# Differential attention: mask first, the two score maps in turn, and a head norm computed in token quarters

## The reference, cut to what matters

```
S_c  = (q_c / 8) k_c^T, causal mask added,   c = 0, 1      # 1024 x 1024, q_c, k_c of width 64
p    = softmax(S_0) - lam * softmax(S_1)
o    = p @ v                                               # width 128
o_a  = o * rsqrt(mean(o*o over the 128) + 1e-6) * gain     # the head norm
y_a  = o_a * silu(z)
```

## Time and profile before

| | us |
|---|---|
| median of 3 runs | 3134.0 (3133.04 to 3135.56) |
| profiled execution, its own time | 3136.14 |
| its span in the profile | 3134.4 |
| TensorE busy | 2935.7 (94%) |
| VectorE busy | 1498.8 (48%) |
| GpSimd busy | 1200.4 (38%) |
| ScalarE busy | 794.3 (25%) |

### The profile page before, as it was taken

One profiled execution on the slowest core, in us unless ns is written; L12 is line 12 of the kernel. 1 busy time (PEld: TensorE's weight loads), 2 busy tenths in 40 slices (PEclk: granted clock), 3 DMA queues, 4 the chain that ended last, 5 costly groups with the idle time before them and its releaser, 6 DMA issues.

```text
span 3134.4 us, 38375 instructions
## 1 busy us (share of the span) xinstructions
PE 2935.7 (94%) x14298; PEld 2324.2 (74%) x14298; DVE 1498.8 (48%) x2235; ACT 794.3 (25%) x1396; POOL 1200.4 (38%) x560
## 2 busy tenths in 40 slices
PE   5899999999979999999997998998879999999997
PEld 2578888888757777777766787877758878888885
DVE  6433433433454556666555655747350134444444
ACT  3410000000053333333332223232233332211212
POOL 0254444444422422122211233334244356565554
PEclk8999999999989999999998999988889999999998
DMA  8111111111111010010100121111222221111112
GB/s 363 61 54 50 50 47 47 47 47 47 41 68 41 22 34 27 27 33 27 33 20 14 41 61 32 48 40 54 81 81 100 81 74 61 60 54 66 54 61 114
DMA packets 58221, 185.24 MB, mean 59 GB/s; under 512 B 17300, under 2 KB 17428, under 8 KB 55976
## 3 DMA queue, kind: packets, MB, share of 16 engines
q1 hardware_dynamic: 37152, 152.68, 14.3%
q10 hardware_dynamic: 21000, 31.61, 2.9%
HBM read 163.22 MB, written 21.05 MB: 59 GB/s over the span
## 4 chain that ended last, share of the span: by engine, by line
PE 81%; DVE 10%; ACT 3%; issue 3%; POOL 1%; DMA 1%; DVEq 0%; POOLq 0%; ACTq 0%; SPq 0%
PE ps L597 26%; PE ps L599 25%; PE ps L598 25%; PE ps L720 1%; PE ps L923 1%; PE ps L665 1%; DVE tree L1746 1%; DVE acc L1864 1%; DVE da_sq L2027 1%; PE ps L771 1%; PE ps L683 1%; DVE ml_t L2133 1%; PE ps L914 1%; DMA edge<-edges 1%; ACT sg_g L1696 0%
## 5 line engine op out<-in xcount | busy, mean ns | idle before, releaser
L458 POOL TENSOR_TENSOR slab_hi<-slab_raw,zero 128x1024 fp32r<-128x1024 f32 x227 | 445.3, 1962 | 1557.7 <-PE ps L599 1466.0
L597 PE MATMUL ps<-h_hi,slab_hi 128*128 128x512 f32 x2512 | 1003.7, 400 | 21.9 <-DVE h_lo L1827 15.5
L598 PE MATMUL ps<-h_lo,slab_hi 128*128 128x512 f32 x2512 | 989.6, 394 | 0.0
L599 PE MATMUL ps<-h_hi,slab_lo 128*128 128x512 f32 x2512 | 989.1, 394 | 0.0
L460 POOL TENSOR_TENSOR slab_lo<-slab_raw,slab_hi 128x1024 fp32r<-128x1024 f32 x227 | 573.0, 2524 | 17.8
L597 PEld LDWEIGHTS ps<-h_hi,slab_hi 128*128 128x128 f32 x2512 | 479.6, 191 | 124.5 <-issue 12.9
L599 PEld LDWEIGHTS ps<-h_hi,slab_lo 128*128 128x128 f32 x2512 | 478.2, 190 | 103.8
L598 PEld LDWEIGHTS ps<-h_lo,slab_hi 128*128 128x128 f32 x2512 | 479.3, 191 | 96.0 <-issue 0.2
L1864 DVE TENSOR_TENSOR acc<-ps,acc 128x512 f32<-128x512 f32 x448 | 295.0, 688 | 55.2 <-PE ps L599 53.3
L1871 DVE TENSOR_TENSOR ffn_p<-ps,ffn_g 128x1024 f32<-128x1024 f32 x22 | 26.9, 1225 | 457.0 <-PE ps L599 449.8
L1862 DVE SCALAR_TENSOR_TENSOR resid<-ps,mod,resid 128x512 f32<-128x512 f32 x320 | 212.5, 744 | 0.0
(11 more groups left out here) (296 smaller groups left out, 4043.0 us busy)
## 6 DMA issues: line engine op xcount, KB each, us to landing
slab_raw<-w_in SPq DMA_DIRECT2D x168, 512.0 KB, 3.5
mod_big<-mod_w SPq DMA_DIRECT2D x12, 2048.0 KB, 13.1
slab_raw<-w_c SPq DMA_DIRECT2D x43, 512.0 KB, 3.5
res_scr<-resid ACTq DMA_DIRECT2D x4, 2048.0 KB, 7.4
resid<-res_scr ACTq DMA_DIRECT2D x2, 4096.0 KB, 12.9
gv_scr<-sg_t ACTq DMA_DIRECT2D x16, 512.0 KB, 2.6
slab_raw<-gv_scr SPq DMA_DIRECT2D x16, 512.0 KB, 3.5
resid<-x_t SPq DMA_DIRECT2D x2, 2048.0 KB, 16.6
```

The lines of the kernel that those rows point to most:

```text
L458: pool.tensor_tensor(hi, raw[slot][:], zeros, ALU.add).then_inc(hi_done.sem, 1)
L597: pe.matmul(dst, w_h, r_h, start=first, stop=False, skip_group_check=True)
L598: pe.matmul(dst, w_h, r_l, start=False, stop=False, skip_group_check=True)
L599: return pe.matmul(dst, w_l, r_h, start=False, stop=last, skip_group_check=True)
```

## The change

- `da_scores`: both waits stand ahead of the tile; then both masks are written first (they now open the accumulation), then for each column chunk the three products, each for map 0 and at once for map 1. The signals of both maps are given by the last two matmuls.
- `da_squares`: four fp32 matmuls with 32 weight columns each, one for each quarter of the tokens; quarter g lands in partitions 32g to 32g+31 of a 256-column area (`norm_stat`: in `PS[1]`'s upper half, in the last head in `PS[2]`). It waits in addition for the value copies of the head (`a_vl`), which read that area.
- `da_root` and `da_norm` work on 128 by 256 (one reciprocal instead of two of 128 by 512).
- `da_spread` is new: four fp32 matmuls, each with one column of the identity repeated as weight, spread the scale over all partitions into the upper halves of `PS[0]` and `PS[1]` (`norm_wide`). It stands behind the first half of the next value projection, ahead of the tile pair's values, and waits for the reciprocal; in the last head's norm it stands between the halves of a projection of the next stage. `da_result` reads PSUM now.
- The wait of the first transposes for the root is gone.

```diff
@@ da_scores (TensorE)
                 cols = slice(i * P, (i + 1) * P)
+                if i >= 1:
+                    pe.wait_ge(a_exp.sem, a_exp.at(h, 2 * (i - 1)))
+                    pe.wait_ge(a_mix.sem, a_mix.at(h, i - 1))
                 for c in range(2):
-                    rows = slice(c * DA_QK, (c + 1) * DA_QK)
-                    if i >= 1 and c == 0:
-                        pe.wait_ge(a_exp.sem, a_exp.at(h, 2 * (i - 1)))
-                    elif i >= 1:
-                        pe.wait_ge(a_mix.sem, a_mix.at(h, i - 1))
-                    for t0 in range(0, (i + 1) * P, HALF):
-                        t1 = min(t0 + HALF, (i + 1) * P)
-                        three(score_bank[c][:, t0:t1], q_hi[rows, cols], q_lo[rows, cols],
-                              k_hi[rows, t0:t1], k_lo[rows, t0:t1], True, True)
-                    pe.matmul(score_bank[c][:, cols], ident_b[:], mask_b[:], start=False, stop=True,
-                              skip_group_check=True).then_inc(a_score.sem, 1)
+                    pe.matmul(score_bank[c][:, cols], ident_b[:], mask_b[:], start=True, stop=False, skip_group_check=True)
+
+                for t0 in range(0, (i + 1) * P, HALF):
+                    t1 = min(t0 + HALF, (i + 1) * P)
+                    diagonal = t1 == (i + 1) * P
+                    for n, (q, k) in enumerate(((q_hi, k_hi), (q_hi, k_lo), (q_lo, k_hi))):
+                        for c in range(2):
+                            rows = slice(c * DA_QK, (c + 1) * DA_QK)
+                            mm = pe.matmul(score_bank[c][:, t0:t1], q[rows, cols], k[rows, t0:t1],
+                                           start=(n == 0 and not diagonal), stop=(n == 2), skip_group_check=True)
+                            if diagonal and n == 2:
+                                mm.then_inc(a_score.sem, 1)
@@ da_squares, da_spread (TensorE)
-            def da_squares(h):
+            def da_squares(h, last=False):
                 pe.wait_ge(a_sq.sem, a_sq.at(h))
                 pe.wait_ge(a_o.sem, a_o.at(h))
-                for t0 in (0, HALF):
-                    mm = pe.matmul(PS[2][:, t0:t0 + HALF], ones[:], da_sq[:, t0:t0 + HALF], start=True, stop=True,
+                if not last:
+                    pe.wait_ge(a_vl.sem, a_vl.at(h + 1))
+                for g in range(4):
+                    mm = pe.matmul(norm_stat(last)[32 * g:32 * g + 32, :], ones[:, 0:32], da_sq[:, g * QUARTER:(g + 1) * QUARTER],
+                                   start=True, stop=True, skip_group_check=True)
+                mm.then_inc(a_ss.sem, 1)
+
+            def da_spread(h, last=False):
+                pe.wait_ge(a_r.sem, a_r.at(h, 0))
+                for g in range(4):
+                    dst = norm_wide(last, g // 2)[:, g % 2 * QUARTER:(g % 2 + 1) * QUARTER]
+                    mm = pe.matmul(dst, ident[:, 32 * g:32 * g + 1].to_broadcast([P, P]), da_rq[:], start=True, stop=True,
                                    skip_group_check=True)
-                mm.then_inc(a_ss.sem, 1)
+                mm.then_inc(a_r.sem, 1)
@@ da_head (TensorE)
                 da_half(h, DA_Z_SLAB, 0 if last else 1)
-                if out:
-                    pe.wait_ge(a_std.sem, a_std.at(h - 1))
                 da_turn(h, 0, 0)
...
                     da_half(h + 1, DA_V_SLAB, 0)
+                if out:
+                    da_spread(h - 1)
                 da_values(h, 0)
@@ behind the last head (TensorE)
-            da_squares(DA_HEADS - 1)
-            project(IN_ML + 1, 1)
-            pe.wait_ge(a_std.sem, a_std.at(DA_HEADS - 1))
+            da_squares(DA_HEADS - 1, last=True)
+            project(IN_ML + 1, 1, between=lambda: da_spread(DA_HEADS - 1, last=True))
@@ da_root (ScalarE)
-                act.activation(da_sq[:], PS[2], ACT.Sqrt, bias=eps[:, 0:1], scale=1.0 / DA_V).then_inc(a_std.sem, 1)
+                act.activation(da_rq[:], norm_stat(last), ACT.Sqrt, bias=eps[:, 0:1], scale=1.0 / DA_V).then_inc(a_std.sem, 1)
@@ da_norm, da_result (VectorE)
-                dve.reciprocal(da_sq[:, half_of(e)], da_sq[:, half_of(e)]).then_inc(a_r.sem, 1)
+                dve.reciprocal(da_rq[:], da_rq[:]).then_inc(a_r.sem, 1)
...
-                dve.wait_ge(a_r.sem, a_r.at(h, e))
-                dve.scalar_tensor_tensor(da_o[:, half_of(e)], da_o[:, half_of(e)], da_gain[:, 0:1], da_sq[:, half_of(e)],
+                dve.wait_ge(a_r.sem, a_r.at(h, 1))
+                dve.scalar_tensor_tensor(da_o[:, half_of(e)], da_o[:, half_of(e)], da_gain[:, 0:1], norm_wide(last, e),
@@ da_head (VectorE)
                     if out and i == 1:
-                        da_norm(h - 1, 0)
+                        da_norm(h - 1)
...
-                    if out and i == 1:
-                        da_norm(h - 1, 1)
```

More of the change, by code:

```diff
@@ L31 @@
 HALF = 512
+QUARTER = 256
 D = 1024
@@ L236, in build @@
         da_o = take("da_o", [P, T])[0]
-        da_sq = take("da_sq", [P, T])[0]
+        da_sq, o_dsq = take("da_sq", [P, T])
+        da_rq = take("da_rq", [P, QUARTER], at=o_dsq)[0]
         y_hi, y_lo = (take(f"da_{n}", [P, T], F32R)[0] for n in ("yh", "yl"))
@@ L273, in build, with norm_stat, norm_wide @@
         PS = [ps[:, n * T:(n + 1) * T] for n in range(4)]
+        def norm_stat(last):
+            return PS[2][:, 0:QUARTER] if last else PS[1][:, HALF:HALF + QUARTER]
+        def norm_wide(last, e):
+            return PS[2][:, half_of(e)] if last else PS[e][:, HALF:T]
         pool_bank = (PS[0], PS[2])
@@ L1471, in da_square, with da_root @@
                     act.activation(da_blocks(da_sq, e, odd), value_blocks[:, :, 1 - odd, :], ACT.Square).then_inc(a_sq.sem, 1)
-            def da_root(h):
+            def da_root(h, last=False):
                 act.wait_ge(a_ss.sem, a_ss.at(h))
-                act.activation(da_sq[:], PS[2], ACT.Sqrt, bias=eps[:, 0:1], scale=1.0 / DA_V).then_inc(a_std.sem, 1)
+                act.activation(da_rq[:], norm_stat(last), ACT.Sqrt, bias=eps[:, 0:1], scale=1.0 / DA_V).then_inc(a_std.sem, 1)
             def da_high(h, e):
@@ L1558, in _ @@
             da_square(DA_HEADS - 1, 1)
-            da_root(DA_HEADS - 1)
+            da_root(DA_HEADS - 1, last=True)
             for e in range(2):
@@ L2023, in da_gate, with da_norm, da_result @@
                        .then_inc(a_o.sem, 1)
-            def da_norm(h, e):
+            def da_norm(h):
                 dve.wait_ge(a_std.sem, a_std.at(h))
-                dve.reciprocal(da_sq[:, half_of(e)], da_sq[:, half_of(e)]).then_inc(a_r.sem, 1)
-            def da_result(h, e):
-                dve.wait_ge(a_r.sem, a_r.at(h, e))
-                dve.scalar_tensor_tensor(da_o[:, half_of(e)], da_o[:, half_of(e)], da_gain[:, 0:1], da_sq[:, half_of(e)],
+                dve.reciprocal(da_rq[:], da_rq[:]).then_inc(a_r.sem, 1)
+            def da_result(h, e, last=False):
+                dve.wait_ge(a_r.sem, a_r.at(h, 1))
+                dve.scalar_tensor_tensor(da_o[:, half_of(e)], da_o[:, half_of(e)], da_gain[:, 0:1], norm_wide(last, e),
                                          ALU.mult, ALU.mult).then_inc(a_y.sem, 1)
@@ L2116, in _ @@
             da_gate(DA_HEADS - 1, 1)
+            da_norm(DA_HEADS - 1)
             for e in range(2):
-                da_norm(DA_HEADS - 1, e)
-            for e in range(2):
-                da_result(DA_HEADS - 1, e)
+                da_result(DA_HEADS - 1, e, last=True)
             for e in range(2):
```

## The result

The changed kernel takes 3091.33 us in the median of 4 runs (3090.89 to 3092.67), the kernel before in the same session 3133.52 (3127.69 to 3135.56, 4 runs): ratio 0.9864, interval 0.9852 to 0.9876. It is 42 us faster; 3094 was forecast. The profiled execution took 3090.89 around a span of 3089.2.

The account below looks back on a forecast made before the run. TensorE, busy 94% of the span, was taken as the bound. Heads 1 to 6 -35.1 us, head 1 +1.3, head 0 -4, head 7 -3, tail +0.6: -40.2 from 3134.0, median 3094; own range 3083 to 3106, whole range 3076 to 3116.

Parts of the forecast that it names:

- Overlap of the row halves: Score tiles on TensorE: both maps' matmuls run side by side, saving 8.4 us a head with the switches.
- X: Time from one map's first score matmul to its mask: 0.48 us for tile 0, 1.59 for tile 7, sum 8.1.
- Norm on TensorE: Head norm: squares -1.2, spread +1.8, wait of tile 2's transposes -0.5, together +0.1 us a head.
- Late terms: Waits after back-to-back maxima: tile 1 0.2, tile 4 0.65, tile 5 0.7, tile 7 0.9; together +2.45 us a head.
- The sum per head: Heads 1 to 6: scores -8.4, norm +0.1, late waits +2.45 us each, six heads together -35.1.
- Head 7: Last head, bound by maxima, exponentials and mixing: gains some 0.3 a tile and part of 1.7 from the reciprocal; -3 us.
- one of the signs of being wrong: Listed signs: pairs starting 0.2 us apart, squares waiting for value copies, clock below 1.00 in heads 2 to 6, spread above 2 us.
- VectorE loses 5 us of reciprocals; both are cover for the next part: Norm step: ScalarE's root falls from 1024 to 256 columns, VectorE loses 5 us; both taken as cover for late waits.
- partial overlap: Rival, score pairs: narrow steps wait for two weight loads in turn, up to 1.5 us a head; 3106, chance 0.13.
- late terms not free: Denies the rival that late waits cost nothing, VectorE being 5 us freer: -17 us more, 3077; chance 0.08.
- The clock case: Rival: TensorE's added waits drop its clock once in each of six heads, 3.7 us a fall, +22; 3116, chance 0.10.
- rival of no overlap: Rival, score tiles: maps run in turn, a tile costs 2X + 0.1, +0.7 us a head; 3139, chance 0.08.

Follow-up runs that it names:

- e9: Kernel before with its own scores, each of its two reciprocals shortened from 512 to 128 columns (the rest left out): 3127.77 us, ratio 0.9972.
- e4: Changed kernel with map 1's row maximum reading only its first 128 columns (part of the computation left out): 3087.40 us, ratio 0.9849.
- e6: Changed kernel with ScalarE's copy of the second query half put ahead of tile 7's exponentials: 3090.41 us, ratio 0.9860.
- e5: Changed kernel with four orders swapped: ScalarE's in tiles 7, 4 and 0 (query copy, squares, transposed copy), VectorE's low parts in tile 4: 3076.71 us, ratio 0.9818.
- e1: Kernel before with the new da_scores alone, keeping its old head norm: 3134.82 us, ratio 1.0002.
- e12: Changed kernel plus one dead VectorE reciprocal of 304 columns a head, ahead of the two subtractions for the low part: 3128.29 us, ratio 0.9987.
- e11: Kernel before with the new scores alone and each of its two reciprocals cut from 512 to 384 columns (the rest left out): 3100.86 us, ratio 0.9899.
- e3: Changed kernel with both masks still first, but map 0's matmuls issued before map 1's instead of alternating: 3095.85 us, ratio 0.9881.
- e10: e5 with the values of tiles 2 and 3 behind the second output half-tile instead of the fifth: 3077.17 us, ratio 0.9814.

## Why the prediction was right, and where its reasons were not

The mechanism that was to save time is the one that did. But the whole gain hung on the order of two instructions that the prediction never looked at, and that this order came out well was luck.

- **Overlap of the row halves: right.** X is unchanged. Tile 7 was 3.38 us from its first matmul to the next work, and 0.20 from the transposes into it; it is 1.79 now, with 0.11. So a tile saves X + 0.08, 8.7 us a head against 8.4.
- **Norm on TensorE: right as a sum (+0.1 forecast, -0.1 measured).** Squares 0.71 against 0.6, spread 1.54 against 1.8 (1245.97 to 1247.51), the tile pair's values behind it 0.82 instead of 0.63 (their length in e9, which has no wait there). The wait that is gone was 0.7 us, not 0.5: values and wait together took 1.32 before, and the 0.52 that the row shows as idle counts from the end of the last matmul. In heads 1 to 6 the squares do not wait for the value copies. The reciprocal took 1.74 against 1.7.
- **Late terms: sizes right, two of four causes wrong.** Tile 1 +0.31 (0.2), tile 4 +0.58 (0.65), tile 5 +0.53 (0.7), tile 7 +0.75 (0.9): 2.17 against 2.45. For tiles 5 and 7 I put it down to the second maximum; by e4 it is not, or hardly. The second exponential follows the first on ScalarE in any case, and the query copy stands behind both (e6), or behind the squares (e5). That the squares stood ahead of the copy was in my text; that it is an order and can be changed was not weighed.
- **The sum per head: -5.85 forecast, -6.35 measured.** -8.7, -0.1 and +2.2 make -6.6; 0.2 come back in steps of 0.05 to 0.07 that the forecast has at nothing, where a score tile or the squares meet other work and no mask stands at the end any more. Head 1 lost 2.5 us of that, not 1.3. Head 7 gained 1.4, not 3: its squares do wait for the value copies, 2.50 us, one of the signs of being wrong, since no projection stands between them there; and its two subtractions do meet the split (1.53 and 2.85 us), so that the outputs behind its tile 4 take 7.54 us instead of 4.29. The tail took 0.8 more, not 0.6. What stands up to the end of head 0 gained 9.1, not 4, but 3.4 of it lie ahead of head 0's first transpose, where runs differ by over 6 us (961.2 to 967.6 over the traces).
- **The step that would have failed: "VectorE loses 5 us of reciprocals; both are cover for the next part".** I summed scores and norm as two terms, -8.4 and +0.1. By that sum the scores alone would have come to about 3094 as well, and they gained nothing. I did not look where `da_yl` stood against GpSimd's split. The norm's part of the change decided all of it, though it saves TensorE nothing. A forecast for the scores alone would have been wrong by 40 us; that the norm alone changes next to nothing, the sum had right.
- **Rivals.** No partial overlap (pairs start within 0.02 us of each other in heads 1 to 6, half of them within 3 ns), late terms not free, the clock stayed at 1.00 in heads 2 to 6. The clock case did occur, in e1 and e12, where two waits of 1.7 to 1.8 us follow each other; a single one of 1.69 left the clock at 1.00 in e11. My rival of no overlap supposed that in turn means one after the other; e3 shows it doesn't. It was also priced too low: it takes 2X + 0.1 for a tile where the main case has 0.26 beside X for masks and switch, and with that it comes to +2.0 a head, 3148, not 3139.

Open: why the clock in head 7 differs between kernels whose waits there are alike. The 0.5 us between e5's and e10's head is read from one trace each.

## What to carry to other kernels

- Two parts of a change can be worth nothing each and 42 us together. Where an instruction with both inputs in SBUF on VectorE runs near a GpSimd operation, list both starts: a term of the sum is only safe if it doesn't change which comes first.
- A saving on TensorE moves what TensorE releases (here GpSimd's split) forward, and not what VectorE's chain releases: look for what they meet on the way.
- When a wait grows after a change, read each engine's order at that place before blaming the instruction that grew: swapping four neighbours gave back 15 us more.

## What the runs showed of the hardware that was not expected

- VectorE's subtraction of 128x512 with both inputs in SBUF takes 0.68 us alone and 1.53 to 2.85 when GpSimd's split started first, ending 0.54 us behind it; GpSimd's takes 2.39 instead of 1.89 when VectorE was first. A lead of 0.04 us decided (before), a lag of 0.09 did (e11).
- Matmuls in rows 0 to 63 and 64 to 127 overlap fully, with 512 columns and with 128, and even when the second's stand three behind in the kernel's order (tile 3 of e3: 0.90 us for both maps, first starts 0.01 apart), so they don't start in that order; a 128-row matmul between them prevents it (tile 0 of the kernel before).
- VectorE's reciprocal is linear in columns: 0.94, 1.74, 2.04, 2.54 and 3.34 us for 128, 256, 304, 384 and 512.
